# Encoder layer on one core: the Fourier stage takes the long sequence first, with its channel factors loaded a stage ahead, and the up projection's first operands are loaded beside the out projection

## The reference, cut to what matters

```python
proj = x @ w_in                                   # 512 Fourier, 512 q, 128 k, 128 v columns
ug = u.reshape(B, S, 4, 128)                      # four Fourier groups of 128 channels
f = jnp.real(jnp.fft.fft2(ug, axes=(1, 3), norm='ortho'))
out = jnp.einsum('bsgc,gcd->bsgd', f, w_fourier)
heads = jnp.concatenate([fourier_mix(u, w_fourier), windowed_attention(q, k, v, sink)], -1)
x = layer_norm(ALPHA * x + heads @ w_out, ...)
h = jnp.square(jax.nn.relu(x @ w_ff1))            # 1024 -> 4096
x = layer_norm(ALPHA * x + h @ w_ff2, ...)
```

## Time and profile before

| | us |
|---|---|
| median of 3 runs (2625.61 to 2626.84) | 2626.43 |
| profiled execution, its own time | 2629.88 |
| its span | 2628.2 |
| PE busy over the span | 2409.4 |
| DVE, ACT, POOL busy | 1598.7, 1097.7, 197.7 |

### The profile page before, as it was taken

The page is one execution under the profiler, slowest core; times in us unless marked ns, Lnnn a source line. Parts: engine busy times, 40 slices in busy tenths (PEclk is TensorE's granted clock), DMA queues, the critical chain, the costliest instruction groups (busy, mean ns, idle before and its releaser), DMA issues. The chain is left out here.

```text
span 2628.2 us, 35335 instructions
## 1 busy us (share of the span) xinstructions
PE 2409.4 (92%) x12192; PEld 2106.7 (80%) x12192; DVE 1598.7 (61%) x2204; ACT 1097.7 (42%) x1746; POOL 197.7 (8%) x251
## 2 busy tenths in 40 slices
PE   4999969499969993999989998998999999999997
PEld 3888858499958883888879998998788888888885
DVE  7545047466646665666666666665545577668666
ACT  2111122488821113444455555554433334444442
POOL 1000020122122220000000000000000010001001
PEclk9999958799989996999999999999999999999998
DMA  7775241532155556555576667664876659877973
GB/s 269 266 260 213 109 161 61 142 81 72 52 174 199 213 192 266 200 215 198 209 271 233 243 241 271 240 236 178 295 258 194 195 165 318 263 226 235 312 226 113
DMA packets 217816, 543.10 MB, mean 207 GB/s; under 512 B 21424, under 2 KB 90032, under 8 KB 198256
## 3 DMA queue, kind: packets, MB, share of 16 engines
q1 hardware_dynamic: 200400, 476.99, 52.0%
q0 software_dynamic: 17312, 64.76, 7.9%
HBM read 361.31 MB, written 180.36 MB: 206 GB/s over the span
## 5 line engine op out<-in xcount | busy, mean ns | idle before, releaser
L1747 DVE TENSOR_TENSOR e_lo<-e_raw,e_hi 128x896 fp32r<-128x896 f32 (+1 forms) x336 | 378.7, 1134 | 265.3 <-ACT e_hi L1730 257.7
L1730 ACT CAST e_hi<-e_raw 128x896 fp32r<-128x896 f32 (+1 forms) x336 | 330.4, 983 | 427.3 <-PE e_bank L64 383.8
L62 PE MATMUL e_bank<-e_hi,e_lo 128*128 128x512 f32 x1120 | 436.6, 390 | 15.7 <-DVE e_lo L1747 15.7
L63 PE MATMUL e_bank<-e_lo,e_hi 128*128 128x512 f32 x1120 | 436.4, 390 | 0.0
L64 PE MATMUL e_bank<-e_hi 128*128 128x512 f32 x1120 | 436.4, 390 | 0.0
L62 PE MATMUL u_bank<-u_x_hi,u_wa_lo 128*128 128x384 f32 (+1 forms) x768 | 275.3, 358 | 50.9 <-DVE u_x_lo L1384 27.6
L63 PE MATMUL u_bank<-u_x_lo,u_wa_hi 128*128 128x384 f32 (+1 forms) x768 | 273.9, 357 | 0.0
L64 PE MATMUL u_bank<-u_x_hi,u_wa_hi 128*128 128x384 f32 (+1 forms) x768 | 273.8, 357 | 0.0
L62 PEld LDWEIGHTS e_bank<-e_hi,e_lo 128*128 128x128 f32 x1120 | 210.8, 188 | 59.8 <-DVE e_lo L1747 16.1
L64 PEld LDWEIGHTS e_bank<-e_hi 128*128 128x128 f32 x1120 | 210.7, 188 | 43.7
L63 PEld LDWEIGHTS e_bank<-e_lo,e_hi 128*128 128x128 f32 x1120 | 210.7, 188 | 43.7
(11 more groups left out here) (183 smaller groups left out, 4256.4 us busy)
## 6 DMA issues: line engine op xcount, KB each, us to landing
u_w_raw<-w_ff SPq DMA_DIRECT2D x48, 1024.0 KB, 7.8
e_raw<-s_t SPq DMA_DIRECT2D x192, 256.0 KB, 3.8
e_raw<-s_h SPq DMA_DIRECT2D x224, 192.0 KB, 2.8
e_raw<-w_ff SPq DMA_DIRECT2D x144, 256.0 KB, 3.8
u_w_sum<-s_ws SPq DMA_DIRECT2D x32, 1024.0 KB, 4.8
e_raw<-s_h SPq DMA_DIRECT2D x112, 256.0 KB, 2.8
s_h<-u_h_sum SPq DMA_DIRECT2D x32, 768.0 KB, 6.9
s_h<-u_h SPq DMA_DIRECT2D x96, 192.0 KB, 2.3
```

What stands on the lines that cost most here:

```text
L62: tensor.matmul(out, w_lo, m_hi, start=first, stop=False, skip_group_check=again)
L63: tensor.matmul(out, w_hi, m_lo, start=False, stop=False, skip_group_check=again)
L1730: act.copy(part(hi, n), part(raw, n)).then_inc(hi_done, 1)
L1747: dve.tensor_tensor(part(lo, n), part(raw, n), part(hi, n).bitcast(F32), ALU.subtract).then_inc(split, 1)
```

## The change

In the Fourier stage the units are now: long sequence with groups 0, 1, 2, then the short sequence with all four groups, then the long sequence with group 3. The short unit is now handled as a whole (one sine copy, one store per unit, not one for each group). `fold` and its roundings work in two halves with a semaphore step each. `chan` and `w_fourier` are loaded by SP during `embed_project`, into memory that both stages hold. The lower parts of the table are taken by DVE (`table_low`), no longer by POOL, and the first unit's `positions` goes over table tiles in its outer loop.

In `mix_out`, the raw `w_out` is loaded into the memory of `mixed` (and one more tile), and after tile 13 POOL issues loads of x blocks 0 to 2 of group 0 and SP loads of slices 0 and 1 of w_ff1, into memory that both stages hold. `mlp_up` then loads only blocks 3 to 6 at its start.

```diff
+    EE, OE, EO, OO = 0, 1, 2, 3
+    units = [(1, (g,)) for g in range(NFG - 1)] + [(0, range(NFG)), (1, (NFG - 1,))]
+    tiles = [(job, i) for job in (1, 0) for i in range(SEQS[job][1] // 4 // P)]
...
             load_unit(0)
-            sp.dma_start(chan[:], chan_d).then_inc(in_ld, 16)
-            sp.dma_start(wf[:], w_fourier.rearrange("g c d -> c g d")).then_inc(in_ld, 16)
-            for n in range(1, len(units) - 1):
+            sp.wait_ge(t_ld[0], 16)
+            for n in range(1, 4):
                 load_unit(n)
...
             load_table(0)
             load_table(1)
-            for n in range(len(tiles)):
-                hi, lo, raw = table(n)
-                pool.wait_ge(t_hi_done, n + 1)
-                pool.tensor_tensor(lo, raw, hi.bitcast(F32), ALU.subtract).then_inc(t_split, 1)
-                if n + 2 < len(tiles):
-                    load_table(n + 2)
+            for i in range(2, len(tiles)):
+                load_table(i)
...
-                dve.tensor_tensor(folded[:, EE:OO + 1, :], half_fold[:, 0, :, :], half_fold[:, 1, :, :], ALU.add)
-                dve.tensor_tensor(folded[:, EO:OE + 1, :], half_fold[:, 0, :, :], half_fold[:, 1, :, :], ALU.subtract
+                dve.tensor_tensor(folded[:, EE, :], half_fold[:, 0, 0, :], half_fold[:, 1, 0, :], ALU.add)
+                dve.tensor_tensor(folded[:, OE, :], half_fold[:, 0, 1, :], half_fold[:, 1, 1, :], ALU.subtract
+                                  ).then_inc(fold_done, 1)
+                dve.tensor_tensor(folded[:, EO, :], half_fold[:, 0, 0, :], half_fold[:, 1, 0, :], ALU.subtract)
+                dve.tensor_tensor(folded[:, OO, :], half_fold[:, 0, 1, :], half_fold[:, 1, 1, :], ALU.add
                                   ).then_inc(fold_done, 1)
...
+            def table_low(i):
+                hi, lo, raw = table(i)
+                dve.wait_ge(t_hi_done, i + 1)
+                dve.tensor_tensor(lo, raw, hi.bitcast(F32), ALU.subtract).then_inc(t_split, 1)
...
             for k in range(KT):
-                sp.dma_start(w_raw[:, k, :], w_out[k * P:(k + 1) * P, :]).then_inc(w_ld[k], 16)
+                sp.dma_start(w_raw[k], w_out[k * P:(k + 1) * P, :]).then_inc(w_ld[k], 16)
...
+                if n == 13:
+                    load_w_first(sp)
...
                 inverse_std(n)
                 if n + 2 < NT:
                     load_x(n + 2)
+                if n == 13:
+
+                    for s in range(2):
+                        pool.wait_ge(mixed_st[s], 32)
+                    load_x_first(pool)
...
-            load_w(0, 0, 0)
-            sp.wait_ge(x_split, 1)
-            load_w(1, 1, 1)
             store_w_sums(0, 0)
...
-                for j in range(NPROD):
+                for j in range(0 if g else NFIRST, NPROD):
...
+        def load_mixing(sp):
+            sp.dma_start(wf[:], d["w_fourier"].rearrange("g c d -> c g d")).then_inc(in_ld, 16)
+            sp.dma_start(chan[:], d["chan"]).then_inc(in_ld, 16)
...
+        def load_w_first(sp):
+            for p in range(2):
+                sp.dma_start(w_first[:, p, :, :], d["w_ff1"][p * P:(p + 1) * P, :].rearrange("p (b c) -> p b c", b=4)
+                             ).then_inc(w_ld[p], 16)
+
+        def load_x_first(pool):
+            for j in range(3):
+                pool.dma_start(x_first[:, j, :].rearrange("p (q c) -> p q c", q=4),
+                             s["xb"][0:4, :, j, :].rearrange("q p c -> p q c")).then_inc(x_ld[j], 16)
```

More of the change, by code:

```diff
@@ new lines, in combine @@
+                for i in range(len(groups)):
+                    end0, o, sin = bias[:, n, i, odd:odd + 1], i * size, sine[:, odd, i, :]
+                    if odd:
+                        cos = bank[:, 6, i * q:i * q + q]
+                        dve.scalar_tensor_tensor(out[:, slot, o + 1:o + half:2], cos, end0, sin[:, 0:q], ALU.add,
+                                                 ALU.subtract)
+                        last = dve.scalar_tensor_tensor(out[:, slot, o + size - 1:o + half:-2], cos, end0, sin[:, 0:q],
+                                                        ALU.add, ALU.add)
+                    for b, at, c, w in () if odd else even_chunks(job, i):
+                        end = min(c + w, q + 1)
+                        dve.scalar_tensor_tensor(out[:, slot, o + 2 * c:o + 2 * end - 1:2],
+                                                 bank[:, b, at:at + end - c], end0, sin[:, c:end], ALU.add,
+                                                 ALU.subtract)
+                        a, end = max(c, 1), min(c + w, q)
+                        top = o + size - 2 * a
+                        last = dve.scalar_tensor_tensor(out[:, slot, top:top - 2 * (end - a) + 1:-2],
+                                                        bank[:, b, at + a - c:at + end - c], end0, sin[:, a:end],
+                                                        ALU.add, ALU.add)
@@ L531, in fold_high @@
             def fold_high(n):
-                act.wait_ge(fold_done, n + 1)
                 if n >= 2:
                     act.wait_ge(z_done, 4 * (n - 1))
-                act.copy(f_hi[:, n % 2, :, :], u_raw[:, n % 2, :].rearrange("p (a b) -> p a b", a=4)
-                         ).then_inc(f_hi_done, 1)
+                folded = u_raw[:, n % 2, :].rearrange("p (a b) -> p a b", a=4)
+                for odd in range(2):
+                    kinds = slice(2 * odd, 2 * odd + 2)
+                    act.wait_ge(fold_done, 2 * n + odd + 1)
+                    act.copy(f_hi[:, n % 2, kinds, :], folded[:, kinds, :]).then_inc(f_hi_done, 1)
             def table_high(n):
@@ L568, in _ @@
             z_high(0, 0)
+            table_high(1)
             z_high(0, 1)
+            table_high(2)
+            table_high(3)
             fold_high(1)
-            for k in range(len(items)):
-                then = next_unit(k)
-                copy_sine(k, 0)
-                if k + 1 < len(tiles):
-                    table_high(k + 1)
-                if then is not None:
-                    copy_bias(then)
-                    z_high(then, 0)
-                if then is not None and then + 1 < len(units):
-                    fold_high(then + 1)
-                copy_sine(k, 1)
-                if then is not None:
-                    z_high(then, 1)
+            for n in range(len(units)):
+                then = n + 1 < len(units)
+                copy_sine(n, 0)
+                if then:
+                    copy_bias(n + 1)
+                    z_high(n + 1, 0)
+                if n + 2 < len(units):
+                    fold_high(n + 2)
+                if n == 1:
+                    table_high(4)
+                copy_sine(n, 1)
+                if then:
+                    z_high(n + 1, 1)
         @block.tensor
@@ L646, in _ @@
             channels(0, 1)
-            for k in range(len(items)):
-                then = next_unit(k)
-                positions(k, 0)
-                if then is not None:
-                    channels(then, 0)
-                positions(k, 1)
-                if then is not None:
-                    channels(then, 1)
+            for n in range(len(units)):
+                then = n + 1 < len(units)
+                positions(n, 0)
+                if then:
+                    channels(n + 1, 0)
+                positions(n, 1)
+                if then:
+                    channels(n + 1, 1)
 def attend(nc, proj_d, sink, bias_d, ident_d, heads_d):
@@ L1053, in mix_out @@
         heads_v = heads_d.rearrange("(k p) t -> p k t", p=P)
+        w_raw = [*(mixed.rearrange("p s j c -> p (s j c)")[:, k * D:(k + 1) * D] for k in range(KT - 1)), w_last[:]]
         block = ctx.enter_context(nc.Block())
@@ L1255, in mlp_up @@
         x_hi = al.sb("x_hi", [P, NPROD, 4, 4, P], F32R)
[L1256 to L1257 removed]
+        x_first, w_raw, x_first_ld, w_ld = first
+        NFIRST = len(x_first_ld)
+        x_rest = al.sb("x_rest", [P, NPROD - NFIRST, 4 * 512])
+        x_lo = [(x_first[:, j, :] if j < NFIRST else x_rest[:, j - NFIRST, :]).rearrange(
+            "p (q k c) -> p q k c", q=4, k=4) for j in range(NPROD)]
         w_sum = al.sb("w_sum", [P, 4, 512])
```

232 lines of the change are left out of this document (120 added, 112 removed).

## The result

| | before | after |
|---|---|---|
| median (lowest to highest), us | 2626.64 (2625.61 to 2628.55) of 4 | 2601.39 (2599.3 to 2601.84) of 4 |
| profiled execution, its own time | 2629.88 | 2601.09 |

The ratio is 0.9898 (95% interval 0.9885 to 0.991), so 1.0% faster; the medians are 25.2 us apart, the two profiled executions 28.8. The page of the changed kernel, its first line, and windows (columns as in the earlier trace rows): the whole Fourier stage before, the same after, and its last part after.

A forecast was written before the change was run, and what follows sets the result against it. PE was taken as busy in nearly all long stages, so gains lie only where it idles or runs at half clock. Fourier 14.8 plus up projection 15.0, others 0, made 29.8 us off the median: 2596.6 us, range 2590 to 2608.

The forecast's parts named there:

- The sum: Whole kernel: Fourier 14.8 plus up projection 15.0, 29.8 us off the profiled 2629.88, giving 2600.1.
- Fourier, 14.8 us: Fourier stage: channels start earlier and PE waits less, ending at 455.1 instead of 469.9; bounds 11 to 18.
- the load of table tile 3: Fourier stage, before the second fold: the last table tile takes 6.6 us from issue to landing.
- Up projection, 15.0 us: Start of the up projection: early x and w_ff1 loads shorten PE's wait; gain 15.0 us, bounds 12 to 16.3.
- now there are four and one store, 15 us, landed at 1017.1. So ACT sets it: Up projection's start: remaining transfers take 3.0 us each and land before ACT's roundings need them, so ACT sets the pace.
- loads still pace the up projection: Up projection's start: POOL's four x loads land too late, costing 0.9 us or more, up to 2604; chance 0.13.
- 13.7 or 16.3: Up projection: gain in us at a later product of its start, with half clock before it or full clock.
- Out projection, 0 us: Out projection: the added x and slice loads cost 0 to 2.3 us, taken as 0.
- no wait for a head's load: Out projection, tile 16: the profile after shows no wait for the heads' load behind the three x loads.
- The clock didn't stay high: Fourier stage rival: clock stays high through short pauses, gain up to 36 us, about 2591; chance 0.09.
- the table ring: Fourier stage rival: late tables or held roundings leave a gain of only 5 to 8 us, 2605; chance 0.08.
- the clock didn't stay at half in the steady part: Fourier stage rival: clock stays at 0.50 for the long units too, kernel slower at 2656; chance 0.02.

The follow-up runs named there:

- e4: The kernel before measured again unchanged, as a control against itself: 2627.97 us, ratio 1.0002.
- e3: The changed kernel measured again, nothing altered: 2600.75 us, ratio 0.9893 against the kernel before.
- e1: The kernel before with only the changed embedding and Fourier stages, out and up projections as before: 2614.94 us, ratio 0.9943.
- e12: The kernel before with only the two mixing factors loaded early, in the embedding stage: 2629.08 us, ratio 1.0004.
- e5: The changed kernel with the two mixing factors loaded late again, in the Fourier stage behind the first unit's load: 2612.63 us, ratio 0.9941 against before.
- e8: The changed kernel with the table subtractions back on POOL instead of DVE: 2602.27 us, ratio 0.9897 against before.

## Why the prediction was right, and where it was off

The direction, the mechanism and both halves came as forecast; the time was 2601.39 us where 2596.6 was said, inside the range of 2590 to 2608.

- **The sum.** On the profiled executions it holds: 2600.1 was worked out and 2601.09 measured; e4's and e3's profiled executions are 2631.09 and 2602.13, 29.0 us apart. The step that was off most is the last one, "off the median it gives **2596.6 us**": the difference between two profiled executions was taken off a median, and 54 executions of the kernel before range from 2624.51 to 2632.61 with a median of 2628.1, 8 of the changed kernel from 2599.04 to 2602.2 with 2601.4. By these the gain is 26.7 us. The 4.8 us from 2596.6 to 2601.4 are 1.0 by which the sum was over the traced gain, 2.1 by which the traced gain is over that of the medians, and 1.7 by which the median of the first three runs, 2626.43, lies under 2628.1. Why before varies by 8 us and after by 3 is open, but for the 2 us told of below.
- **Luck in it.** The traced gain of 28.8 us, stage by stage, is -1.7 ahead of the Fourier stage (variation, by the ends of the input projection above), 17.0 in it, 0.1 in attention and out projection, 14.3 in the up projection and -0.8 behind it. A Fourier half that won more than its 14.8 stands beside small losses elsewhere that the sum had at 0, and of the 14.3 some 2 us are not the change's (below). That the sum is right to 1 us is luck; that both halves lie within their bounds is not.
- **Fourier, 14.8 us (bounds 11 to 18).** 16.5 in the profile of after, to the last sine copy. The points, behind the first issue, as said and as measured: first channels 12.3 and 11.6, table 3's issue 22.9 and 22.7, landed 29.6 and 27.7, second unit's channels 40.5 and 38.6, last sine copy 113.3 and 111.55. The mis-sized term is the load of table tile 3, 6.6 us said and 5.0 measured. The half clock came as counted, over the second unit's channels (382.1 to 391.0), though not behind the 2.77 us wait, where the products ran at full: products of 512 columns went from 0.63 to 0.39 us here.

```profile
390.18 0.63 PE L65 MATMUL b_bank<-b_t_hi,b_z_hi 128*128 128x512 f32 x1
...
391.50 0.39 PE L63 MATMUL b_bank<-b_t_hi,b_z_lo 128*128 128x512 f32 x1
```

- **That load and its page.** The row's 6.6 us and the 7.15 of the sum by the page are both above the 5.0 measured, so the measurement decides. The Trainium skill, "DMA: Bandwidth & Descriptors", has 6.15 us for 1 MB issued by GpSimd in "Bandwidth" and about 1 us to the first byte in "Latency and other measured facts"; the 5.0 us, which hold the issue too, are under the first alone.
- **Up projection, 15.0 us (bounds 12 to 16.3).** P1 8.5 said, 8.07 measured. P2 18.9 said, 20.8 measured: the step "now there are four and one store, 15 us, landed at 1017.1. So ACT sets it" failed. The last of the four blocks, with the 1 MB store beside them, landed after 18.4 us and not 15, 3.7 us each and not 3.0, so ACT waited 2.16 us for block 6. The rival "loads still pace the up projection" had this wait with a price of 0.9 us at 4.3 us a block; the wait came, with 1.9 at P2. P5 gained 12.0 us, at the lower bound, where the middle of P5's gain was the stage's forecast: it stands 5.04 us behind P2, at half clock as before, so of "13.7 or 16.3" it was the smaller, less P2's 1.9. By the up projection's last product 14.3 were gained (1829.0 - 1002.04 before, 1799.4 - 986.70 after). Of these, 12.2 stand at the wait for P1's copy in the second group of tokens and the other 2.1 only at that of the third, before and then after:

```profile
1346.65 0.69 PE L62 MATMUL u_bank<-u_x_hi,u_wa_lo 128*128 128x384 f32 x1 [5.77 <-ACT u_p L1527]
...
1595.53 0.69 PE L62 MATMUL u_bank<-u_x_hi,u_wa_lo 128*128 128x384 f32 x1 [5.82 <-ACT u_p L1527]
```

```profile
1319.07 0.69 PE L63 MATMUL u_bank<-u_x_hi,u_wa_lo 128*128 128x384 f32 x1 [5.67 <-ACT u_p L1571]
...
1565.89 0.69 PE L63 MATMUL u_bank<-u_x_hi,u_wa_lo 128*128 128x384 f32 x1 [5.82 <-ACT u_p L1571]
```

  Behind the first issue these stand at 344.6 and 593.5 before, 332.4 and 579.2 after: 12.2 us gained at the one, 14.3 at the other. The change touches nothing between them, and e1 shows that the 2.1 us are not its work: with the up projection of before it has 247.0 us from the one wait to the other (e12 247.6), as after has 246.8, where before and e4 have 248.9 and 248.8. The first products behind DVE's sums in the second group differ, in before and then in e1:

```profile
1360.64 0.44 PE L62 MATMUL u_bank<-u_x_hi,u_wb_lo 128*128 128x384 f32 x1 [1.85 <-DVE u_c L1455]
...
1363.69 0.52 PE L63 MATMUL u_bank<-u_x_lo,u_wb_hi 128*128 128x384 f32 x1
```

```profile
1347.02 0.45 PE L63 MATMUL u_bank<-u_x_hi,u_wb_lo 128*128 128x384 f32 x1 [1.51 <-DVE u_c L1487]
...
1348.71 0.33 PE L63 MATMUL u_bank<-u_x_hi,u_wb_lo 128*128 128x384 f32 x1
```

  Behind the pause of 1.85 us (1.87 in e4) the products run at half clock for some 3 us, behind that of 1.51 (1.48 in after) they don't. So the change's own part of this stage is 12.2 us (11.8 from e4 to e3), at the lower bound of the forecast: its term of 15.0 was 3 us too high, by P2's wait for the loads and by the clock behind P2, and a stretch of half clock in the traces of before hid it.

- **Out projection, 0 us.** The cost was right, but "no wait for a head's load" was not: the load of tile 16's heads took 13.2 us behind the three x loads, and ACT waited for it, as its timeline in after shows (and 5.16 us more for tile 18's). PE did not wait: 13.2 us are under the 16.5 that the earlier trace rows allow, and the window over the place has it busy throughout.

```profile
916.54 1.05 ACT L1161 CAST d_h_hi<-d_h_raw 128x1024 fp32r<-128x1024 f32 x1 [7.08 <-DMA d_h_raw<-s_heads]
```

```profile
916.00:930.00 14.00, 14.00 (x68) 11.67 (x67) 10.21 (x13) 3.07 (x4) 3.10 (x4) 1.00 0.74 264
```

- **Embedding stage, 0 us.** Right, by the six ends above.
- **The other rivals.** The clock didn't stay high (half from 382.1 to 391.0), the table ring gave no 5 us back, and the clock didn't stay at half in the steady part: the windows show 1.00 from 402 to 455. The Trainium skill, "TensorE: Matmul & The Clock Gate", "Seeing it yourself", tells of a gate stuck at a quarter of the clock for over 50 us; no row here shows a quarter, and the dense products of the steady part ran at full.
- **What the prediction didn't see.** It priced the Fourier half as one chain and was right in that, but its list reads as if the early factors and the new order each gave a part. By e5 and e12 the loads alone give nothing and the order alone 4.5 us; together they give 17.0. Nor has its sum a term for the clock, which is 7.0 of the 17.0 us; before, PE ran at half up to 408.5, as this window has it:

```profile
341.83:408.50 66.67, 41.25 (x172) 37.64 (x173) 40.77 (x60) 20.95 (x28) 19.93 (x10) 0.50 0.44 150
```

## What to carry to other kernels

A load moved ahead paid only where the engine that consumes it also took it early: look at what stands before the consumer in its queue, on every engine down to the one that waits. Behind a stage's barrier, an instruction that is short and wanted early (here P1's copy) should not stand behind one that waits for a transfer. And a gain worked out from one trace should be compared with a trace, and its translation to a median given the spread of the kernel's executions as an error of its own.

## What the runs showed of the hardware

- A POOL subtraction of 2050 columns, which reads and writes on-chip memory, held a DVE addition of two such operands for its whole length, 5.0 us for 0.68, twice in e8. By the Trainium skill, "SBUF — State Buffer", section "Who interferes with whom", the two engines share a pair of ports; where a DVE operation has two SBUF inputs and the POOL operation reads SBUF, the one issued second is fully blocked until the first is done. The trace agrees. In the kernel before, the same showed as the 3.72 us row. DVE operations with one input in `b_bank`, where PE's results stand, took their usual 0.69 us beside a POOL subtraction (`b_z_lo`, at 363.64 and 366.20 in e8).
- Four loads of 1 MB issued together by POOL, with a store of 1 MB by SP 2.8 us behind, took 18.4 us until the last load had landed; one load alone took 5.0 us.
- Small loads issued behind large ones landed late: `chan`, 128 KB, landed 11.9 us behind the stage's first issue in e5, beside 1 MB of the sequence and two table tiles.
- The granted clock fell behind short pauses, and not behind all of them: in the up projection's second group a pause of 1.85 us was followed by some 3 us of products at half clock and one of 1.51 us by none; in the Fourier stage of after, 2.77 us by none, and 4.89 us shortly behind it by 8.9 us at half.
